# Latent projections inside the loop over the attention heads, and the latent rotary work on GpSimd

## What is computed

```python
mod = silu(c) @ w_ada + b_ada            # six vectors of 2048: shifts, scales, gates
h = rms_norm(x, g_norm1) * (1 + sc1) + sh1
proj = h @ w_in                          # q_d, k_d, v_d, cq (512), ckv (256), k_pe (64)
q_d, k_d = rms_norm(q_d, g_q_diff), rms_norm(k_d, g_k_diff)
# differential: two maps of 64 a head, with a bias by distance
p = softmax(q_d @ k_d.T * 64 ** -0.5 + bias)
a_out = (p[0] - lam * p[1]) @ v_d
# latent: heads of 192, the last 64 rotary
q_m = rms_norm(cq, g_q_a) @ w_q_b        # 256 x 8 x 192
kv = rms_norm(ckv, g_kv_a) @ w_kv_b      # 256 x 8 x (128 + 128)
k_m = concatenate([k_nope, k_pe for all heads])
q_m, k_m = rope_tail(rms_norm(q_m, g_q_mla)), rope_tail(rms_norm(k_m, g_k_mla))
b_out = softmax(q_m @ k_m.T * 192 ** -0.5) @ v_m
x = x + gt1 * (concatenate([a_out, b_out]) @ w_out)
```

## Time and profile before

| | us |
|---|---|
| median of 3 runs (2476.35 to 2481.53) | 2476.92 |
| the profiled execution | 2476.22 |
| its span, first to last instruction | 2474.5 |
| TensorE busy | 2346.9 (95%) |
| VectorE, ScalarE, GpSimd busy | 845.7, 1030.1, 1389.7 |
| mean granted TensorE clock | 0.98 |

### The profile page before, as it was taken

One profiled execution on the slowest core, in us unless ns is written; L12 is line 12 of the kernel. 1 busy time (PEld: TensorE's weight loads), 2 busy tenths in 40 slices (PEclk: granted clock), 3 DMA queues, 4 the chain that ended last, 5 costly groups with the idle time before them and its releaser, 6 DMA issues.

```text
span 2474.5 us, 30054 instructions
## 1 busy us (share of the span) xinstructions
PE 2346.9 (95%) x10876; PEld 1856.7 (75%) x10876; DVE 845.7 (34%) x1318; ACT 1030.1 (42%) x1276; POOL 1389.7 (56%) x660
## 2 busy tenths in 40 slices
PE   5889979998999999999999999999999999999987
PEld 2566644677888888888877887778888888888775
DVE  3344565554111122222235897521111111111234
ACT  3233354444344444444445444444444444444433
POOL 1101111004888888888882000058888888888776
PEclk9999999999999999999999999999999999999999
DMA  8979987554565555555656554556666655556553
GB/s 348 365 286 354 356 304 283 192 180 136 185 189 189 193 187 193 188 189 192 189 176 212 170 188 137 182 188 193 189 194 188 191 191 188 193 188 190 166 162 127
DMA packets 131269, 513.94 MB, mean 208 GB/s; under 512 B 14464, under 2 KB 20224, under 8 KB 118272
## 3 DMA queue, kind: packets, MB, share of 16 engines
q1 hardware_dynamic: 116800, 411.88, 51.5%
q0 software_dynamic: 13824, 100.67, 10.5%
q10 hardware_dynamic: 576, 0.47, 0.1%
HBM read 510.86 MB, written 2.10 MB: 207 GB/s over the span
## 4 chain that ended last, share of the span: by engine, by line
PE 88%; DVE 6%; ACT 2%; DMA 2%; POOL 1%; issue 1%; DVEq 0%; SPq 0%; ACTq 0%; POOLq 0%
PE ps L1776 81%; PE ps L1797 3%; POOL w_lo L836 1%; DMA ada_raw<-in_w_ada 1%; DVE w_lo L1225 1%; PE ps L1694 1%; DMA raw<-in_w_in 1%; PE ps L1743 1%; PE ps L1945 0%; DVE fm_lo L1200 0%; PE ps L1922 0%; ACT w_hi L601 0%; PE ps L1921 0%; DVE row_max L1457 0%; ACT fm_hi L620 0%
## 5 line engine op out<-in xcount | busy, mean ns | idle before, releaser
L836 POOL TENSOR_TENSOR w_lo<-raw,w_hi 128x1024 fp32r<-128x1024 f32 x554 | 1334.0, 2409 | 484.7 <-ACT w_hi L601 484.7
L601 ACT ACTIVATE w_hi<-raw 128x1024 fp32r<-128x1024 f32 x766 | 809.2, 1058 | 1279.4 <-PE ps L1776 1258.6
L1776 PE MATMUL ps<-w_hi,fm_hi 128*128 128x512 f32 (+1 forms) x2176 | 858.3, 394 | 28.6 <-DVE fm_lo L1267 14.3
L1776 PE MATMUL ps<-w_hi,fm_lo 128*128 128x512 f32 (+1 forms) x2176 | 850.0, 391 | 0.0
L1776 PE MATMUL ps<-w_lo,fm_hi 128*128 128x512 f32 (+1 forms) x2176 | 849.8, 391 | 0.0
L1776 PEld LDWEIGHTS ps<-w_hi,fm_hi 128*128 128x128 f32 x2176 | 411.7, 189 | 142.5 <-issue 35.9
L1776 PEld LDWEIGHTS ps<-w_lo,fm_hi 128*128 128x128 f32 x2176 | 411.7, 189 | 85.9
L1776 PEld LDWEIGHTS ps<-w_hi,fm_lo 128*128 128x128 f32 x2176 | 411.9, 189 | 82.4
L1225 DVE TENSOR_TENSOR w_lo<-raw,w_hi 128x1024 fp32r<-128x1024 f32 (+1 forms) x212 | 256.5, 1219 | 221.3 <-ACT w_hi L601 218.0
L1776 PE MATMUL ps<-w_hi,hid_hi 128*128 128x512 f32 x704 | 275.1, 391 | 5.5 <-issue 5.5
L1776 PE MATMUL ps<-w_lo,hid_hi 128*128 128x512 f32 x704 | 274.5, 390 | 0.0
(11 more groups left out here) (263 smaller groups left out, 1258.8 us busy)
## 6 DMA issues: line engine op xcount, KB each, us to landing
ada_raw<-in_w_ada POOLq DMA_DIRECT2D x96, 1024.0 KB, 7.9
raw<-in_w_gate SPq DMA_DIRECT2D x176, 512.0 KB, 3.4
raw<-in_w_up SPq DMA_DIRECT2D x176, 512.0 KB, 3.4
raw<-in_w_down SPq DMA_DIRECT2D x176, 512.0 KB, 3.4
raw<-in_w_in SPq DMA_DIRECT2D x120, 512.0 KB, 3.8
raw<-in_w_out SPq DMA_DIRECT2D x64, 512.0 KB, 3.5
raw<-in_w_ple_gate SPq DMA_DIRECT2D x32, 512.0 KB, 3.5
raw<-in_w_q_b SPq DMA_DIRECT2D x6, 512.0 KB, 5.8
```

The source lines that it names most:

```text
L601: act.activation(w_hi[:, hi_slot, :, 0:width], raw[:, slot, :, 0:width], ACT.Copy).then_inc(hi_ready, 1)
L836: pool.tensor_tensor(w_lo[:, slot, :, 0:width], raw[:, slot, :, 0:width], w_hi[:, hi_slot, :, 0:width], ALU.subtract).then_inc(lo_ready, 1)
L1776: last = pe.matmul(banks[t][:, 0:width], a, b, start=kt == 0 and k == 0, stop=kt == kts - 1 and k == 2)
```

## The change

Three things change together.

1. The order of the projections. All 32 pieces of the modulation groups 4 and 5 are multiplied in the input projection, one at a time behind four pieces of five, where 26 of them stood there in pairs and six between the latent query units. The latent units, now the four of `w_kv_b` (k 0 to 3) and then the three of `w_q_b` (k 4 to 6), are multiplied in steps 0 to 4 of the head loop: k 0 and 1 in step 0, 2 and 3 in step 1, then one a step. All use PSUM banks 2 and 3, so the logits of the differential heads use banks 0 and 1 alone, and head `n` waits until VectorE has read the logits of head `n-1`. ScalarE's copies and splits and VectorE's low parts go with them, two pieces a step.
2. The latent rotary work. GpSimd turns and scales the keys once VectorE has `rstd` (step 2), and turns the queries once the last unit is copied. The queries are no longer scaled: their reciprocal roots go into `q_scale`, which is the scale operand of the exponentials and of the maxima. Their sums come from ScalarE's squares with an accumulator, head by head, in steps 5 and 6.
3. The transfers. SyncE issues the gate pieces (64 to 95) within its own list of steps, and the first two bias tables before the first latent piece. Four operand tiles lie elsewhere in SBUF.

```diff
+STREAM = [(8 + u, "kv_b", u, 1) for u in range(4)] + [(12 + u, "q_b", u, 2) for u in range(3)]
+AFTER_LOGITS = {0: 0, 1: 2, 2: 4, 3: 5, 4: 6}
+AT_END = {0: 1, 1: 3}
+STREAM_STEPS = 5
+
+
+def stream_end(k):
+    return FIRST["kv_b"] + sum(pieces for _, _, _, pieces in STREAM[:k + 1])
...
-        cq_hi = at("cq_hi", 176.75, [P, 4, S], F32R)
-        cq_lo = at("cq_lo", 180.75, [P, 4, S], F32R)
-        ckv_hi = at("ckv_hi", 184.75, [P, 2, S], F32R)
-        ckv_lo = at("ckv_lo", 186.75, [P, 2, S], F32R)
+        cq_hi = at("cq_hi", 193, [P, 4, S], F32R)
+        cq_lo = at("cq_lo", 102, [P, 4, S], F32R)
+        ckv_hi = at("ckv_hi", 106, [P, 2, S], F32R)
+        ckv_lo = at("ckv_lo", 170, [P, 2, S], F32R)
...
-            for p in range(FIRST["out1"] + RAW):
+            def ada(n):
+                sp.wait_ge(ada_used, n - ADA + 1)
+                sp.dma_start(ada_raw[:, n % ADA, :], io["w_ada"][n]).then_inc(gate_piece_landed[n % ADA], 16)
+
+            for p in range(FIRST["kv_b"] + RAW):
+                if p == FIRST["kv_b"]:
+                    bias_load(0)
+                    bias_load(1)
                 weights(p)
-
-            bias_load(0)
-            bias_load(1)
-            for h in range(2, HEADS):
-                sp.wait_ge(bias_used, h - 1)
-                bias_load(h)
+            for h in range(2 * HEADS):
+                ada(ADA_FIRST[G_GATE] + 2 * h)
+                ada(ADA_FIRST[G_GATE] + 2 * h + 1)
+                if h + 2 < HEADS:
+                    sp.wait_ge(bias_used, h + 1)
+                    bias_load(h + 2)
+                if h < STREAM_STEPS:
+                    weights(FIRST["kv_b"] + RAW + 2 * h)
+                    weights(FIRST["kv_b"] + RAW + 2 * h + 1)
 
...
+            def copy_latent(k):
+
+                r, name, u, _ = STREAM[k]
+                act.wait_ge(pieces_used, stream_end(k))
+                dst = (q_mla if name == "q_b" else kv_mla)
+                for t in range(TT):
+                    last = act.activation(dst[:, t, :, :].rearrange("p h d -> p (h d)")[:, u * NW:(u + 1) * NW],
+                                          ps[:, 2 + t, :], ACT.Copy)
                 last.then_inc(unit_read, 1)
...
+                if s in AFTER_LOGITS:
+                    copy_latent(AFTER_LOGITS[s])
                 if s >= 1:
                     copy_mix(s - 1)
-                if s == 2:
-                    splits(FIRST["out1"], FIRST["out1"] + AHEAD)
+                if s in AT_END:
+                    copy_latent(AT_END[s])
+                if s < STREAM_STEPS:
+                    splits(FIRST["kv_b"] + AHEAD + 2 * s, FIRST["kv_b"] + AHEAD + 2 * s + 2)
+                if s == 1:
+                    act.wait_ge(unit_read, 12)
+                    for t in range(TT):
+                        act.activation(y[:, t, 1024:2048].rearrange("p (h d) -> p h d", h=HEADS), kv_mla[:, t, :, 0:NOPE], ACT.Square)\
+                           .then_inc(squares, 1)
+                if s in (5, 6):
+                    t = s - 5
+                    act.wait_ge(unit_read, 15)
+                    act.wait_ge(squares, 4 + t)
+                    for h in range(HEADS):
+                        junk = slice(1024 + h // 2 * QK, 1024 + (h // 2 + 1) * QK)
+                        last = act.activation(y[:, h % 2, junk], q_mla[:, t, h, :], ACT.Square,
+                                              accum_out=ssq[:, 8 * t + h:8 * t + h + 1])
+                    last.then_inc(squares, 1)
...
-                            src, scale = ps[:, 2 * (n % 2), t * S:(t + 1) * S], QK ** -0.5
+                            src, scale = ps[:, 2 * (n % 2), t * S:(t + 1) * S], q_scale[:, t, n - HEADS:n - HEADS + 1]
...
+            def mla_operands():
+
+                half, steps = ROPE // 2, [0]
+
+                def stepped(ins):
+                    steps[0] += 1
+                    ins.then_inc(mla_step, 1)
+                    pool.wait_ge(mla_step, steps[0])
+
+                def rope_gains(g):
+                    cos, sin = cs[:, :, 0:half], cs[:, :, half:ROPE]
+                    g1 = g[:, 0:half].unsqueeze(1).to_broadcast([P, TT, half])
+                    g2 = g[:, half:ROPE].unsqueeze(1).to_broadcast([P, TT, half])
+                    for k, (a, b) in enumerate(((cos, g1), (sin, g2), (cos, g2), (sin, g1))):
+                        last = pool.tensor_tensor(turn[:, k, :, 0:half], a, b, ALU.mult)
+                    stepped(last)
+
+                def spread(width, t):
+                    return rstd[:, 16 + 8 * t:24 + 8 * t].unsqueeze(2).to_broadcast([P, HEADS, width])
+
+                pool.wait_ge(mla_rstd, 1)
+                rope_gains(gk_rope)
+                rt = rope_t[:, :, 0:TT * half].rearrange("p a (t c) -> p a t c", t=TT)
+                k1, k2 = lat[:, :, 768:768 + half], lat[:, :, 768 + half:832]
+                for o, (a, b, op) in enumerate((((k1, 0), (k2, 1), ALU.subtract), ((k2, 2), (k1, 3), ALU.add))):
+                    pool.tensor_tensor(rt[:, 0], a[0], turn[:, a[1], :, 0:half], ALU.mult)
+                    stepped(pool.tensor_tensor(rt[:, 1], b[0], turn[:, b[1], :, 0:half], ALU.mult))
+                    stepped(pool.tensor_tensor(rope_k[:, :, o * half:(o + 1) * half], rt[:, 0], rt[:, 1], op))
+                for t in range(TT):
+                    pool.tensor_tensor(k_pe[:, t, :, :], rope_k[:, t, :].unsqueeze(1).to_broadcast([P, HEADS, ROPE]),
+                                       spread(ROPE, t), ALU.mult)
+                    pool.tensor_tensor(kv_mla[:, t, :, 0:NOPE], kv_mla[:, t, :, 0:NOPE], spread(NOPE, t), ALU.mult)
+                rope_gains(gq_rope)
+                pool.wait_ge(unit_read, 15)
+                rt = rope_t[:, :, :].rearrange("p a (h c) -> p a h c", h=HEADS)
+                for t in range(TT):
+                    x1, x2 = q_mla[:, t, :, NOPE:NOPE + half], q_mla[:, t, :, NOPE + half:QK]
+                    for o, (a, b, op) in enumerate((((x1, 0), (x2, 1), ALU.subtract), ((x2, 2), (x1, 3), ALU.add))):
+                        pool.tensor_tensor(rt[:, 0], a[0], turn[:, a[1], t, 0:half].unsqueeze(1).to_broadcast([P, HEADS, half]), ALU.mult)
+                        stepped(pool.tensor_tensor(rt[:, 1], b[0], turn[:, b[1], t, 0:half].unsqueeze(1).to_broadcast([P, HEADS, half]),
+                                                   ALU.mult))
+                        stepped(pool.tensor_tensor(q_pe[:, t, :, o * half:(o + 1) * half], rt[:, 0], rt[:, 1], op))
+                pool.sem_inc(mla_ready, 1)
+
...
-            for n in range(ADA, ADA_PIECES):
+            for n in range(ADA, ADA_FIRST[G_GATE]):
                 ada(n)
...
+                if s < STREAM_STEPS:
+                    for p in range(FIRST["kv_b"] + AHEAD + 2 * s, FIRST["kv_b"] + AHEAD + 2 * s + 2):
+                        rest(p)
                 if s >= 2:
                     read_pv(s - 2)
-                if s == 3:
-                    for p in range(FIRST["out1"], FIRST["out1"] + AHEAD):
-                        rest(p)
-
-                if s == 1:
+                if s == 2:
                     latent_sums()
-                if s == 2:
-                    mean_to_rstd(32, QK)
-                    rope_keys()
-                if s in (3, 4):
-                    scale_latent(s - 3)
-                if s in (4, 5):
-                    rope_queries(s - 4)
+                    mean_to_rstd(16, QK, 16)
+                    dve.sem_inc(mla_rstd, 1)
+                if s == 7:
+                    dve.wait_ge(squares, 6)
+                    mean_to_rstd(16, QK)
+                    link(dve.tensor_scalar(q_scale[:, :, :].rearrange("p t h -> p (t h)"), rstd[:, 0:16], QK ** -0.5, None, ALU.mult))
...
-                    dve.tensor_scalar(row_max[:, q, 0:2], row_max[:, q, 0:2], QK ** -0.5, None, ALU.mult).then_inc(maxes, 1)
+                    dve.tensor_tensor(row_max[:, q, 0:2], row_max[:, q, 0:2], q_scale[:, :, n - HEADS], ALU.mult).then_inc(maxes, 1)
...
-                if p % 3 == 2:
+                while n < ADA_FIRST[G_SHIFT2] + 4 * (p + 1 - 6 * QUARTERS) // 5:
                     ada(n)
-                    ada(n + 1)
-                    n += 2
+                    n += 1
                 if p == in1_end(3) - 1:
...
+            def latent_unit(k):
+
+                r, name, u, pieces = STREAM[k]
+                pe.wait_ge(unit_read, r)
+                hi, lo = (cq_hi, cq_lo) if name == "q_b" else (ckv_hi, ckv_lo)
+                product(hi, lo, PK * pieces, FIRST[name] + pieces * u, (ps[:, 2, :], ps[:, 3, :]),
+                        operand_after=OPERANDS["c" + name[:-2]] if u == 0 else None)
 
...
-                    pe.wait_ge(mla_ready, TT)
-                    pe.wait_ge(maxes, HEADS - 1)
+                    pe.wait_ge(mla_ready, 1)
+                    pe.wait_ge(unit_read, 15)
...
-                if n >= 2:
+                if n == 0:
+                    pe.wait_ge(unit_read, 7)
+                elif n <= HEADS:
```

(7 more changed lines are left out.)

130 lines of the change are left out of this document (34 added, 96 removed).

## The result

The changed kernel takes 2486.49 us (median of 6 runs, 2481.93 to 2487.64) against 2476.64 for the kernel before (6 runs, 2474.47 to 2481.53). The ratio is 1.003, with a 95% interval of 1.0019 to 1.0042: slower, by 9.9 us going by the medians and by 7 (5 to 10) going by the ratio. The profiled execution took 2487.44 (span 2485.7) against 2476.22 (span 2474.5), so 11.2 us more. Forecast were 2484.3 and a mark B near 413.

A forecast was written before the change was run, and what follows sets the result against it. TensorE bounds the kernel, waiting in the changed region for the ring of VectorE and ScalarE. 10.6 + (99.0 - 109.6) + 2.0 + 6.1 = +8.1 on 2476.2 gives 2484.3 us; own range 2480 to 2489, 8-in-10 range 2469 to 2492.

The forecast's parts named there:

- mark B: TensorE's transposes for head 10, the third latent one, at 405.40 us before; what moves it was said to move the end.
- Term 1: Input projection: 32 modulation pieces one at a time instead of 26 in pairs put A 10.6 us later.
- A: The first matmul on the latent query weights, at 295.77 us before; start of the region the change touches.
- Term 2: From A to mark B without disturbance: the chain of latent units and heads takes 99.0 us against 109.6 before.
- Term 3: Behind TensorE's 4.9 us wait in the head loop, half speed loses 2.0 us (bounds 0 and 4).
- Term 4: Between A and mark B, GpSimd's two-input instructions slow VectorE's low parts and `combine` by 6.1 us (bounds 0 and 9).
- the rival of its coming last: GpSimd's query rotation becomes the last, from 1.7 us an instruction on: 8.5 us more, 2493; chance 0.08.
- Gate pieces, "hidden": SyncE issues them in the head loop some 11 us ahead, 2.6 MB before them taking 7 us: no cost.
- The step from B to the end: Behind mark B TensorE is busy without a gap, so what moves that mark moves the end.
- The faster rival: Half of TensorE's 17.2 us of waits in steps 0 to 4 gone, no clock or interference cost: 2467.6; chance 0.17.

The follow-up runs named there:

- the four edits: Changed kernel with modulation pieces paired, gate pieces ahead of units 1 and 3 and issued ahead of the bias load, low parts behind `combine`: 2467.12 us, 0.996.

## Why the prediction was right, and where its parts were not

The time was 2.2 us above the forecast and inside its own range (2480 to 2489), and it was slower, as forecast. Taken term by term:

- **Term 1** (+10.6 to A): +10.0 measured, 11.4 for all 32 in the kernel before, 6.3 back for pairs. Right, mechanism and size.
- **Term 2** (plain chain of 99.0 from A to B): 109.4 measured, less 4.8 for the clock behind the waits before units 1 and 3, 3.2 for GpSimd and 3.0 for the gate piece, leaves 98.4. Waits of 2.8 and 4.9 were 2.74 and 4.60, that of 2.9 was 3.41, that of 1.5 did not come, and that of 5.1 was 5.68 with one of 2.26 behind it. `combine` of head 0, whose end was forecast at 19.2, ended at 21.8 with 2.4 of clock in it. That 98.4 is so near to 99.0 is partly luck: the transposes and the pair behind the waits of 5.68 and 2.26 lost 0.5 and 1.7 us at half speed, where the prediction had such a loss absorbed; in the run with the gate pieces first TensorE waits less than 0.5 us at a time from there to B, so the loss is on the path. Against it, steps 6 (less those 3.0) and 7 took 5.5 and 6.2 us, where 7.0 to 7.5 were forecast. The squares were put at 0.40 and took 0.35:

```profile
L805 ACT ACTIVATE y<-q_mla x16: 347/350/355, 394.0 to 403.0; 128x192 f32<-128x192 f32 x16
```
- **Term 3** (clock, +2.0): mis-sized. Both waits cost 2.4 us, the 2.74 one too, so 4.8, a little over the upper bound of 4. What was wrong in it is the choice of what is lost on the path: the loss was read from a pair and four transposes, but what follows here is a unit of 3.0 us, on which the chain hangs, and it is slow as a whole. The loss differs between executions: 1.2 and 1.5 in the one without GpSimd's arithmetic, nothing behind 3.22 us with the four edits.
- **Term 4** (GpSimd, +6.1): mis-sized the other way, 3.2 by the rows and at most 5. The 3.31 against 1.23 of the earlier trace rows stand for 1024-column instructions on both sides. Here GpSimd's instructions are of 256 columns, and the low parts lost 0.67 of the 3.4 allowed. `combine` lost more than the 1.2 allowed, 2.3. The Trainium skill (SBUF — State Buffer, section "SBUF: two separate sides") has GpSimd's instructions, and VectorE's with two SBUF inputs or in a 2-port mode, take a shared port pair for one instruction at a time, the other being blocked until it ends. By that a VectorE instruction loses at most what is left of one of GpSimd's, here of 0.72 us; the two pairs in `combine` lost 0.5 and 0.4 an instruction, a low part up to 0.5, so these rows agree. GpSimd paid as well: 

```profile
380.88 0.72 POOL L898 TENSOR_TENSOR rope_t<-q_mla,turn 128x256 f32<-128x256 f32 x1
381.68 1.64 POOL L900 TENSOR_TENSOR q_pe<-rope_t 128x256 f32<-128x256 f32 x1
```
  It was done at 391.2 and asked for at 402, so the rival of its coming last was rightly small. The 0.7 us an instruction that were forecast hold where VectorE leaves it alone.
- **Gate pieces, "hidden"**: wrong, 3.0 us. The working counted the bytes ahead of them (7 us of 11), not the wait ahead of them: SyncE stands at the bias load until VectorE has added the bias of the head.
- **The step from B to the end**, "what moves B moves the end": not so for a few microseconds, as the two runs with a delay show. It rested on TensorE being busy without a gap from B on, and the trace of before has waits of 7.58 us at 558.22, 3.02 at 1282.90 and 7.93 at 2360.93, with stages at either clock behind them. Here 1.4 us came behind B.

So two errors of about 3 us each, term 3 and the gate pieces, were mostly set off by term 4 and by half a microsecond each of terms 1 and 2. The direction rests on terms 1 and 2, which the runs bear out; that the sum came out within 2.2 us is partly luck. The faster rival (waits shrink by half, 2467.6) did not come true in the changed kernel. One order edit on VectorE halves the waits it names (2.76, 2.69 and 3.05, together 8.5 in place of 17.2), but new ones for gate pieces stand behind them and the time is 2475.9. The rival's condition was put at ScalarE's copy; the runs put it at VectorE, whose low parts waited for ScalarE ahead of work that was ready.

## What to carry to other kernels

Where an engine works through one list, look at what each wait holds up: two low parts ahead of `combine`, a gate piece behind a bias load and squares ahead of `combine` cost 12, 3 and 6 us at mark B, and each was an order, not work. Fill a wait of TensorE with work that is due anyway, since behind a wait of 3 us the next 3 us of matmuls can take 5.4 (they need not: in two traces they took 2.9). And judge an edit of a few microseconds by a mark right behind it before judging it by the end of a long program.

## What the runs showed of the hardware

- Behind a wait of 2.74 us TensorE's 128x512 matmuls came every 0.43 us instead of 0.23, for 5.4 us, and the granted clock of the window 306 to 325 was 0.82; with the wait filled it was 1.00. Behind a wait of 3.22 us at the same place of the program, with the four edits, they came every 0.23 us.
- Beside GpSimd's 256-column instructions two of VectorE's 128x256 ones in a row went from 0.61 to 1.69 us, while a 1024-column low part lost 0.1 to 0.5, and the bias add, which reads PSUM, none (1.21 at 389.05).
- One and the same stage took 216.1, 217.8 or 219.4 us in the traces of 14 kernels, and 20 useless transposes made the kernel with the early bias tables 4.1 us faster.
